# A two-layer trunk with expert lookups on one core: the latents' projection and layer 1's modulation change places, the prompt's ranking runs beside its queries, latents go in groups of 1, 1 and 2, and attention's copies move to ScalarE

## The chip, the cores and the metric

One NeuronCore of a Trainium2 chip runs the whole program. The metric is the device time of one execution in microseconds (us); the median of the runs counts. Engines: TensorE (PE, with its weight load PEld), VectorE (DVE), ScalarE (ACT), GpSimd (POOL) and SyncE (SP). SP and POOL issue transfers; 16 DMA engines carry them.

## The reference, cut to what matters

There are 5 tiles of 128 tokens: tile 0 is the prompt, tiles 1 to 4 are the latents. Both of the two layers run this sequence for every tile:

```python
m = silu(cond) @ w_mod + b_mod            # 6 rows of 1024: shift, scale, gate, shift, scale, gate
h = rms_norm(x) * (1 + scale) + shift
layer 0: p = h @ l0_w_in                  # 2080 columns: q, k, v, r, decay inputs, pool inputs
         y = concat(gla(p), pool(p)) @ l0_w_out
layer 1: q, k, v = h @ l1_w_in            # 1536 columns
         y = window_attention(q, k, v)    # 16 heads, +-128 tokens, cached context, a sink logit
x = x + gate * y                          # (layer 1: y is attention's output @ l1_w_out)
h = rms_norm(x) * (1 + scale2) + shift2   # PEER, the expert lookup:
s = (h @ w_q) . keys                      # 8 heads x 2 halves x 128 keys
top 16 of each half, top 16 of their sums # 128 experts a token, with softmax gates
act = gelu(u[expert] . h);  x = x + gate2 * sum(gates * act * v[expert])
```

GLA of a latent tile needs the states of all latent tiles, so the projection of all four comes before any of them is mixed.

## The kernel before, in words

**Experts in the background.** `Experts` keeps one sequence of 10 x 128 slots: layer, tile, and one of 128 experts per token. For each slot GpSimd issues an indirect DMA (L1928) that fetches 128 rows of 8 KB (`u` and `v` together) into a ring of 8 buffers (9 in layer 1). VectorE takes the dot product with `h` (L1945), ScalarE makes gelu, gate and, for slots that TensorE owns, a diagonal matrix (L1968, L1971, L1974); then either VectorE adds the weighted row (L1960) or TensorE does (L1985, `sum_rows`). A buffer is free again after that. GpSimd can't gather a tile before its selection is done: it waits on `selected`.

**Foreground and rates.** Everything else is a row of stages in program order. Each stage has units, and a rate tuple (rate, places on TensorE, lead). On entry the goal of processed slots rises by lead, and after unit u it stands at base + int(u x rate); every engine's program puts the slots' steps at those places. `bg.allow(n)` cuts the goal off at n x 128 slots. Before the first selection there are no slots, and the same mechanism (`core.fill = early`) fills the prolog with the steps of `Early`.

**The order before.** `modulation_stage` does the first 4 of 12 chunks of layer 0's modulation. Then come the prompt's norm, projection, decays, GLA, pool, output projection (`p0_out`), queries and selection. Beside them `Early` does 8 more chunks of layer 0's modulation (L358, L2135, L2149, L2156; weights by GpSimd, L2185) and then the norm (L2240, L2241, L2249) and the projection (L2262, L2226) of all four latent tiles. When both are done, the background starts. The latents' decays, GLA and pool of tile 1, its output projection, queries and selection (`s0a`) follow; then the same for tiles 2 to 4 together (`s0b`), with one pass over the weights `l0_w_out` and `peer_wq` and three selections. Then `mod1` does layer 1's modulation in 12 chunks. In layer 1 the prompt and tiles 1 and 2 are normed and projected together (`j1`), then come attention and the selections for the prompt and tile 1, and so on (`s1b`, `s1c`).

**Two details.** A selection (`select_stage`, 21 units) makes 16 score matmuls (L1748) and ranks all 16 rows in five passes (L1774 to L1782), then pairs and ranks the sums. In attention VectorE takes a head's maximum (L1638), negates it (L1645), ScalarE exponentiates (L1618), TensorE transposes (L1582), VectorE copies the transposed tile out of PSUM (L1652), and TensorE multiplies with the values (L1594). A pair of heads goes through at a time, with the background's slots between maxima and copies.

The main sequence of layer 0 before:

```python
early.finish()
core.fill = bg
bg.allow(1)
latent_decay_stage(core, "s0_decay", latents, pr, la, st, ahead, FIRST_RATES["decay"])
layer0_mix(core, "s0a", latents, [0], pr, la, st, constants, (BAND_FIRST, BAND_AFTER), FIRST_RATES)
first_experts(core, "s0a", first, 0, FIRST_RATES, None, 2, env["h"][:, others[0], :])
bg.allow(2)
layer0_mix(core, "s0b", latents, [1, 2, 3], pr, la, st, constants, (BAND_AFTER, BAND_BEFORE), REST_RATES)
other_experts(core, "s0b", latents[1:], 0, 1, REST_RATES)
```

## Time and profile before

| what | value |
|---|---|
| median of 3 runs | 4137.85 us (4133.88 to 4142.95) |
| profiled execution, its time | 4151.75 us |
| its span, first to last instruction | 4149.6 us |
| busy: PE, DVE, ACT, POOL | 2942.8, 3047.3, 1414.3, 1613.3 us |
| moved by DMA | 1521.91 MB, mean 367 GB/s |
| of it by the gathers' queue (q0) | 1366.06 MB |
| granted TensorE clock, mean | 0.848 |

A profile is one execution. The time minus the span (2 us) lies around the first and last instruction. Busy shares are means over stages with different limits, so they don't tell what a stage waits for. The granted clock is TensorE's share of 2.4 GHz.

### The profile page before, as it was taken

The numbers are of one execution on the slowest core, as the hardware profiler recorded it, in microseconds if no ns is written. First come the engines' busy times: TensorE is split into PE (matmuls) and PEld (weight loads), VectorE is DVE, ScalarE is ACT, GpSimd is POOL, SyncE is SP. The second block draws the span as 40 slices with busy tenths as digits, with TensorE's granted clock in tenths as the row PEclk, the third lists the DMA queues.
The fourth block names the chain that finished last, engine by engine and source line by source line (L and its number), as shares of the span: only waits on it lengthen the run. The fifth ranks groups of instructions, "written<-read, shape, count | busy, mean of one in ns | idle before, by whom it ended". The sixth has DMA issues, their size and how long they took to land.

```text
span 4149.6 us, 32638 instructions
## 1 busy us (share of the span) xinstructions
PE 2942.8 (71%) x9247; PEld 1520.7 (37%) x9247; DVE 3047.3 (73%) x6149; ACT 1414.3 (34%) x4109; POOL 1613.3 (39%) x1309
## 2 busy tenths in 40 slices
PE   6699756875877844757768877776787677755665
PEld 2365342444522311423446323344355533222222
DVE  1406779978897847697778886978797898666666
ACT  1213323522233312235522332542464233332222
POOL 0001332434544524344333553434544454444443
PEclk8798887987999966877879988888998899888888
DMA  9143897989998999899999999999999999999998
GB/s 363 57 169 144 330 397 271 344 338 357 416 393 368 396 404 382 329 396 404 366 381 403 406 382 390 385 386 419 411 408 410 419 407 381 422 422 414 418 422 365
DMA packets 222322, 1521.91 MB, mean 367 GB/s; under 512 B 29757, under 2 KB 33537, under 8 KB 48822
## 3 DMA queue, kind: packets, MB, share of 16 engines
q0 software_dynamic: 186912, 1366.06, 81.3%
q1 hardware_dynamic: 35230, 153.77, 9.4%
q8 instruction: 74, 1.21, 0.1%
q14 instruction: 106, 0.87, 0.1%
HBM read 1516.49 MB, written 3.24 MB: 366 GB/s over the span
## 4 chain that ended last, share of the span: by engine, by line
DMA 29%; PE 29%; DVE 24%; issue 8%; POOL 4%; ACT 4%; DVEq 1%; SPq 1%; PEldq 0%; PEld 0%; ACTq 0%
DMA core_ring<-in_l_uv,core_experts 24%; PE sum_rows L1985 7%; DVE core_ring L1945 7%; DVE core_yv L1960 5%; POOL core_ring L1928 4%; PE sum_rows L2262 2%; PE j_in_ps L490 2%; PE s1c_query_pq L1699 1%; PE s1b_in_ps L490 1%; DMA s0a_h_w<-in_l_peer_wq 1%; DMA layer_slot<-in_l_uv,core_experts 1%; PE j_query_pq L1699 1%; DMA mod_w<-in_l_w_mod 1%; PE s0b_out_po L629 1%; DVEq L159 1%
## 5 line engine op out<-in xcount | busy, mean ns | idle before, releaser
L1928 POOL DMA_INDIRECT core_ring<-in_l_uv,core_experts x1209 | 1515.2, 1253 | 2111.3 <-PE sum_rows L1985 974.9
L1985 PE MATMUL sum_rows<-core_ring,core_diag 128*128 128x512 f32 x2820 | 1533.8, 689 | 600.6 <-ACT core_diag L1974 477.1
L1945 DVE CUSTOM_DVE_ANT_0 core_ring<-core_ring,core_hc 128x1024 f32<-128x1024 f32 x1209 | 1465.0, 1223 | 583.0 <-DMA core_ring<-in_l_uv,core_experts 408.3
L1985 PEld LDWEIGHTS sum_rows<-core_ring,core_diag 128*128 128x128 f32 x2820 | 576.1, 217 | 1482.6 <-ACT core_diag L1974 792.2
L1968 ACT ACTIVATE core_wt<-core_wt 128x1 f32<-128x1 f32 x1280 | 256.3, 200 | 1660.0 <-DVE core_wt L1945 1566.8
L1960 DVE SCALAR_TENSOR_TENSOR core_yv<-core_ring,core_wt,core_yv 128x1024 f32<-128x1024 f32 x494 | 632.7, 1281 | 22.6 <-ACT core_wt L1971 22.1
L1971 ACT ACTIVATE core_wt<-core_wt,core_gates 128x1 f32<-128x1 f32 x1280 | 376.8, 294 | 41.6
L1974 ACT ACTIVATE core_diag<-core_ident,core_wt 128x128 f32<-128x128 f32 x705 | 283.1, 401 | 23.0
L1985 PE MATMUL sum_rows<-layer_slot,layer_diag 128*128 128x512 f32 x184 | 107.6, 715 | 44.8 <-ACT layer_diag L1974 34.0
L2262 PE MATMUL sum_rows<-core_ring 128*128 128x416 f32 x320 | 117.8, 528 | 5.2 <-DVEq L159 4.1
L1945 DVE CUSTOM_DVE_ANT_0 layer_slot<-layer_slot,core_hc 128x1024 f32<-128x1024 f32 x71 | 86.9, 1224 | 44.0 <-DMA layer_slot<-in_l_uv,core_experts 29.8
L1928 POOL DMA_INDIRECT layer_slot<-in_l_uv,core_experts x71 | 84.4, 1188 | 85.7 <-DVE core_yv L1960 40.6
L1968 ACT ACT_TABLE_LOAD x81 | 103.9, 1283 | 5.2 <-DVEq L159 3.8
L1945 DVE DVE_READ_ACCUMULATOR2_ANT core_wt<- 128x1 f32 x1280 | 104.4, 82 | 0.0
L1699 PE MATMUL s0b_query_pq<-s0b_h_hT,s0b_h_w 128*128 128x384 f32 x256 | 85.3, 497 | 5.4 <-DVEq L159 5.4
L2262 PEld LDWEIGHTS sum_rows<-core_ring 128*128 128x128 f32 x320 | 61.8, 196 | 57.3 <-issue 57.1
L2194 POOL DMA_DIRECT2D core_ring<-in_l_w_in x5 | 2.7, 536 | 206.1 <-PE sum_rows L2262 206.1
L1985 PEld LDWEIGHTS sum_rows<-layer_slot,layer_diag 128*128 128x128 f32 x184 | 38.5, 222 | 107.7 <-ACT layer_diag L1974 59.7
L358 PE MATMUL mod_pm<-mod_w,mod_c_silu 128*32 128x512 f32 x192 | 45.8, 972 | 38.0 <-DMA mod_w<-in_l_w_mod 38.0
L490 PE MATMUL j_in_ps<-j_in_w,j_atth_hT 128*128 128x384 f32 x192 | 65.1, 504 | 5.8 <-DMA j_in_w<-in_l_w_in 5.8
L1699 PE MATMUL j_query_pq<-s_att_pr,j_h_w 128*128 128x256 f32 x256 | 59.8, 393 | 8.1 <-DVEq L159 7.8
L1699 PEld LDWEIGHTS s0b_query_pq<-s0b_h_hT,s0b_h_w 128*128 128x128 f32 x256 | 49.8, 195 | 40.8 <-issue 8.2
(778 smaller groups left out, 3293.4 us busy)
## 6 DMA issues: line engine op xcount, KB each, us to landing
mod_w<-in_l_w_mod SPq DMA_DIRECT2D x16, 2048.0 KB, 12.5
core_ring<-in_l_uv,core_experts POOLq DMA_INDIRECT x1209, 11.9
core_ring<-in_l_w_mod POOLq DMA_DIRECT2D x6, 2048.0 KB, 11.0
s_mix_pr<-in_l_w_in SPq DMA_DIRECT2D x5, 1664.0 KB, 11.0
core_ring<-in_l_w_in POOLq DMA_DIRECT2D x5, 1664.0 KB, 10.5
p_h_w<-in_l_peer_wq SPq DMA_DIRECT2D x16, 512.0 KB, 4.5
s0a_h_w<-in_l_peer_wq SPq DMA_DIRECT2D x16, 512.0 KB, 12.9
s0b_h_w<-in_l_peer_wq SPq DMA_DIRECT2D x16, 512.0 KB, 8.0
```

Source lines behind the costliest of these rows:

```text
L159: dve.drain().then_inc(meeting, 1)
L358: mm = nc.tensor.matmul(out[lo:lo + 32, :], silu[:, k, :], w[:, k, :], start=(k < 4), stop=(k >= 4))
L490: mm = nc.tensor.matmul(ps[:, i % 4, 0:chunk], hT[:, k, t * P:(t + 1) * P], w[n % 2][:, k * chunk:(k + 1) * chunk], start=(k == 0), stop=( ...
L1699: mm = nc.tensor.matmul(pq[:, n % 2, 0:tok], queries.chunk(n)[:, k, :], hT[:, k, :], start=(k == 0), stop=(k == DK - 1))
L1928: nc.gpsimd.indirect_dma_start(self.slots[r], None, core.a[f"l{layer}_uv"], bass.IndirectOffsetOnAxis(ap=self.experts[:, t, n:n + 1], axis ...
L1945: nc.vector.tensor_tensor_reduce(self.slots[r][:, 0:D], self.slots[r][:, 0:D], self.hc[:], 1.0, 0.0, ALU.mult, ALU.add, self.wt[:, r:r + 1 ...
L1960: x = nc.vector.scalar_tensor_tensor(self.yv[:], self.slots[r][:, D:], self.wt[:, r:r + 1], self.yv[:], ALU.mult, ALU.add)
L1968: nc.scalar.activation(self.wt[:, r:r + 1], self.wt[:, r:r + 1], ACT.Gelu_apprx_tanh).then_inc(self.gelu_done, 1)
L1971: nc.scalar.activation(self.wt[:, r:r + 1], self.wt[:, r:r + 1], ACT.Copy, scale=gate).then_inc(self.wt_done, 1)
L1974: nc.scalar.activation(self.diags[r], self.core.env["ident"][:], ACT.Copy, scale=self.wt[:, r:r + 1]).then_inc(self.diag_done, 1)
L1985: mm = nc.tensor.matmul(self.py[:, c * 512:(c + 1) * 512], self.diags[r], self.slots[r][:, D + c * 512:D + (c + 1) * 512], start=(at == 0) ...
L2262: mm = nc.tensor.matmul(self.ps[:, i % 2 * 512:i % 2 * 512 + self.CH], self.hT[:, k, t * P:(t + 1) * P], w[:, k, :], start=(k == 0), stop= ...
```

## The change

- `Early` no longer norms and projects the latents. It does 20 chunks of modulation: layer 0's last 8 and all 12 of layer 1. `mod1` is gone. Readers of layer 1's rows wait for them (`wait_rows`).
- The latents' norm and projection are ordinary stages (`layer0_rows`, `s0`) after the background has started, in the slots of tile 0, with rates of their own.
- The prompt's selection: `query_stage` makes the scores of a half head right behind its queries and ranks four rows at a time; the selection has 16 units left.
- Latents in layer 0 go as tile 1, tile 2 (`s0b`, by `first_experts`), tiles 3 and 4 (`s0c`), so `l0_w_out`, `peer_wq` and the keys are loaded three times for the latents and not twice.
- In attention the copy of the transposed tile is ScalarE's, behind its background slots of the pair; it was VectorE's.
- Rates of the prolog and of layer 0 are set anew.

```diff
@@ attention_stage, scalar
+            def take_turned(n):
+                keys, _ = keys_of(which[n // QH])
+                act.wait_ge(tr_done, n + 1)
+                if n >= 2:
+                    act.wait_ge(o_mm, n - 1)
+                nc.scalar.activation(pT[:, n % 2, 0:len(keys), :], ptr[:, n % 2, 0:len(keys), :], ACT.Copy).then_inc(pT_done, 1)
...
                 if n % 2:
                     s.tick("scalar", act, n + 1)
+                    take_turned(n - 1)
+                    take_turned(n)
@@ attention_stage, vector
-            def take_turned(n):
...
-                take_turned(n)
-                take_turned(n + 1)
@@ query_stage, tensor
+            def score(n):
+                if n == 0:
+                    pe.wait_ge(keys_in, 32)
+                pe.wait_ge(qT_done, n + 1)
+                nc.tensor.matmul(ranking.scores[:, n, :], qT[:, n, 0:P], keys[:, n * NKEYS:(n + 1) * NKEYS], start=True, stop=True
+                                 ).then_inc(ranking.scored, 1)
...
+                if n and ranking:
+                    score(n - 1)
@@ query_stage, vector
+            def rank(first):
+                rows = range(first, first + ROWS_AT_ONCE)
+                dve.wait_ge(ranking.scored, first + ROWS_AT_ONCE)
...
+                if ranking and n >= ROWS_AT_ONCE + 1 and (n - 1) % ROWS_AT_ONCE == 0:
+                    rank(n - 1 - ROWS_AT_ONCE)
+            if ranking:
+                rank(HC - ROWS_AT_ONCE)
@@ Early
-    MOD_STEPS, MOD_FIRST, MOD_CH, MOD_CHUNKS = 11, 4, 512, 12
-    STEPS = MOD_STEPS + 29
+    MOD_FIRST, MOD_CH, MOD_CHUNKS = 4, 512, 12
...
+        self.chunks = [(0, n) for n in range(self.MOD_FIRST, self.MOD_CHUNKS)] + [(1, n) for n in range(self.MOD_CHUNKS)]
+        self.rows = [(layer, n // 2) for layer, n in self.chunks[::2]]
+        self.STEPS = len(self.chunks) + 3
@@ Early.load, gpsimd
+            for n in range(2, chunks):
+                pool.wait_ge(self.mod_mm, n - 1)
+                pool.dma_start(self.mod_w[n % 2], self.weights(n)).then_inc(self.mod_w_in[n % 2], 16)
+                if n >= 5 and n % 2:
+                    store((n - 5) // 2)
+            for i in range(len(self.rows) - 2, len(self.rows)):
+                store(i)
+            for i in range(len(self.rows)):
+                pool.wait_ge(self.stored[i], 16)
@@ rates
-EARLY_RATES = {"norm": (0.0, None, 0), "in": (1.6, None, 2), "decay": (1.0, None, 1), "gla": (1.0, None, 1), "pool": (1.0, None, 1),
-               "out": (0.5, None, 2), "query": (0.0, None, 0), "select": (0.6, None, 1)}
+EARLY_RATES = {"norm": (0.0, None, 0), "in": (1.6, None, 2), "decay": (1.0, None, 1), "gla": (0.65, None, 0), "pool": (1.0, None, 0),
+               "out": (0.34, None, 1), "query": (0.0, None, 0), "select": (0.15, None, 0)}
-FIRST_RATES = {"norm": (2.0, PE_4, 5), "decay": (2.0, PE_8, 0), "gla": (1.6, PE_6, 4), "pool": (2.0, PE_2, 4),
-               "out": (1.7, PE_0, 3), "query": (1.0, PE_0, 2), "select": (0.8, PE_8, 3)}
-REST_RATES = {"norm": (3.0, PE_4, 5), "gla": (2.0, PE_6, 4), "pool": (2.0, PE_2, 4), "out": (1.75, PE_0, 3), "query": (2.0, PE_0, 2),
-              "first select": (1.5, PE_8, 3), "select": (2.1, PE_8, 3)}
+FIRST_RATES = {"norm": (2.0, PE_4, 5), "in": (1.9, PE_0, 4), "decay": (2.0, PE_8, 0), "gla": (1.6, PE_6, 4), "pool": (2.0, PE_2, 4),
+               "out": (1.7, PE_0, 3), "query": (1.0, PE_0, 2), "select": (1.1, PE_8, 3)}
+SECOND_RATES = {"gla": (2.0, PE_6, 4), "pool": (2.0, PE_2, 4), "out": (1.9, PE_0, 3), "query": (1.15, PE_0, 2), "select": (1.8, PE_8, 3)}
+REST_RATES = {"gla": (2.0, PE_6, 4), "pool": (2.0, PE_2, 4), "out": (1.9, PE_0, 3), "query": (1.25, PE_0, 2),
+              "first select": (2.0, PE_8, 3), "select": (2.1, PE_8, 3)}
@@ program
-            ahead = Ahead(core, latents)
-            first_experts(core, "p0", 0, 0, EARLY_RATES, ahead)
+            first_experts(core, "p0", 0, 0, EARLY_RATES, ranked=True)
             early.finish()
             core.fill = bg
             bg.allow(1)
+            ahead = Ahead(core, latents)
...
+            layer0_rows(core, "s0", latents, pr, None, (), FIRST_RATES, ahead.load)
...
-            layer0_mix(core, "s0b", latents, [1, 2, 3], pr, la, st, constants, (BAND_AFTER, BAND_BEFORE), REST_RATES)
-        other_experts(core, "s0b", latents[1:], 0, 1, REST_RATES)
-        with Stage(core, "mod1_c") as m:
-            modulation_stage(core, 1, "mod1", m.sb("silu", [P, DK, 32])[:], early.MOD_CHUNKS, [1, 4], 2, (2.5, PE_0, 3))
+            layer0_mix(core, "s0b", latents, [1], pr, la, st, constants, (BAND_AFTER, BAND_BEFORE), SECOND_RATES)
+            first_experts(core, "s0b", latents[1], 0, SECOND_RATES, 2, env["h"][:, latents[2], :])
+            bg.allow(3)
+            layer0_mix(core, "s0c", latents, [2, 3], pr, la, st, constants, (BAND_AFTER, BAND_BEFORE), REST_RATES)
+        other_experts(core, "s0c", latents[2:], 0, 2, REST_RATES)
```

## Rows read from the trace of the kernel before

**Rows 1.** The page: GB/s moved in 40 equal slices of the span.

```profile
GB/s 363 57 169 144 330 397 271 344 338 357 416 393 368 396 404 382 329 396 404 366 381 403 406 382 390 385 386 419 411 408 410 419 407 381 422 422 414 418 422 365
```

**Rows 2.** Busy time by stretch: length, each engine, clock, DMA share, GB/s.

```profile
0.00:373.00 373.00, 292.61 (x1257) 165.43 (x1258) 107.74 (x322) 64.75 (x109) 11.97 (x26) 0.87 0.44 169
276.00:306.00 30.00, 29.19 (x257) 28.66 (x256) 0.00 (x0) 4.43 (x16) 0.00 (x0) 1.00 0.65 215
373.00:423.00 50.00, 41.38 (x164) 24.11 (x163) 30.35 (x54) 33.05 (x61) 19.02 (x18) 0.76 0.83 317
423.00:500.00 77.00, 54.49 (x257) 28.39 (x255) 61.81 (x102) 31.67 (x73) 22.86 (x21) 0.86 0.80 303
500.00:615.00 115.00, 68.86 (x352) 54.48 (x352) 78.82 (x102) 26.77 (x88) 39.58 (x32) 0.81 0.98 400
615.00:692.00 77.00, 49.27 (x105) 19.20 (x106) 74.95 (x267) 23.46 (x71) 24.49 (x20) 0.80 0.82 311
692.00:872.00 180.00, 140.40 (x691) 70.68 (x690) 160.83 (x276) 87.74 (x194) 59.99 (x52) 0.91 0.81 307
1450.00:1655.00 205.00, 87.51 (x268) 22.82 (x267) 118.20 (x161) 38.77 (x128) 69.83 (x49) 0.67 0.97 395
1655.00:1705.00 50.00, 34.42 (x67) 15.25 (x66) 30.21 (x42) 21.26 (x48) 14.07 (x12) 0.65 0.58 219
1705.00:1780.00 75.00, 66.05 (x195) 37.90 (x193) 51.80 (x66) 15.48 (x56) 32.67 (x24) 0.95 1.01 423
1780.00:2095.00 315.00, 216.48 (x592) 108.14 (x593) 259.88 (x465) 160.62 (x447) 138.13 (x116) 0.77 0.96 388
2095.00:2250.00 155.00, 114.34 (x446) 87.00 (x444) 113.46 (x142) 38.76 (x118) 54.16 (x45) 0.84 0.98 391
2250.00:2370.00 120.00, 94.00 (x215) 40.21 (x216) 103.92 (x317) 45.65 (x147) 60.49 (x47) 0.93 0.99 399
2370.00:2500.00 130.00, 100.55 (x220) 41.36 (x219) 107.54 (x320) 45.76 (x148) 65.38 (x49) 0.89 0.97 390
3600.00:4050.00 450.00, 276.31 (x445) 95.84 (x446) 304.07 (x430) 133.93 (x470) 212.05 (x179) 0.83 1.01 419
```

**Rows 3.** The chain that ended last, 300 to 373.5 us: start, length.

```profile
315.59 55.88 PE sum_rows L2262 x160
```

**Rows 4.** Groups of instructions, 0 to 373 us: busy us, mean ns | idle before.

```profile
L2262 PE MATMUL sum_rows<-core_ring 128*128 128x416 f32 x320 | 117.8, 528 | 5.2 <-DVEq L159 4.1 <-ACTq L154 0.6 <-PEq L164 0.5
...
L358 PE MATMUL sum_rows<-core_ring 128*32 128x512 f32 x128 | 18.2, 641 | 5.0 <-DMA core_ring<-in_l_w_mod 2.6 <-ACTq L154 1.4 <-ACT core_ring L2149 1.0
...
L2240 DVE SCALAR_TENSOR_TENSOR core_h<-core_x,core_wt,core_ring 128x1024 f32<-128x1024 f32 x4 | 5.1, 1284 | 0.1
```

**Rows 5.** Instructions in order of time, end of the prolog: start, length.

```profile
315.63 3.26 DVE L1774 MAX8 p_select_vals<-p_select_pscore 128x8 f32<-128x128 f32 x16 [8.06 <-PE p_select_pscore L1748]
...
335.22 0.29 DVE L1790 CAST p_select_idxf<-p_select_i 128x256 f32<-128x256 uint32 x1
...
361.03 0.29 DVE L1836 TENSOR_TENSOR core_gates<-p_select_ts,p_select_gs 128x128 f32<-128x128 f32 x1
...
373.15 1.00 POOL L1928 DMA_INDIRECT core_ring<-in_l_uv,core_experts  x1 [45.36 <-issue]
```

**Rows 6.** The page: DMA issues, KB each, median us from issue to landing.

```profile
core_ring<-in_l_uv,core_experts POOLq DMA_INDIRECT x1209, 11.9
...
s0a_h_w<-in_l_peer_wq SPq DMA_DIRECT2D x16, 512.0 KB, 12.9
```

**Rows 7.** Waits, 3000 to 3190 us: us in total, times, longest.

```profile
ACT s1c_attend_sc L1618 <- DVE s1c_attend_mx L1645: 40.8, 16, 6.8
```

**Rows 8.** Groups of instructions, 3000 to 3190 us: busy us, mean ns.

```profile
L1652 DVE COPY s1c_attend_pT<-s1c_attend_ptr 128x512 f32<-128x512 f32 (+1 forms) x32 | 18.3, 613 | 0.0
...
L1618 ACT ACTIVATE s1c_attend_sc<-s1c_attend_sc,s1c_attend_mx 128x512 f32<-128x512 f32 (+1 forms) x32 | 21.4, 669 | 40.8 <-DVE s1c_attend_mx L1645 40.8
...
L1618 ACT ACT_TABLE_LOAD x16 | 20.5, 1283 | 5.0 <-DVE s1c_attend_mx L1645 4.7
```

281 lines of the change are left out of this document (124 added, 157 removed).

## The prediction

> **What bounds the kernel now.** I read the page's row of bytes moved first: after the first tenth of the span the DMA engines move 330 to 420 GB/s nearly everywhere, and only the start has holes [rows 1]. Then busy time by stretch, in stretches cut at the stages: in the free-running end 179 gathers take 450 us at 419 GB/s and a DMA share of 1.01, so one slot (128 expert rows, 1.05 MB) costs 2.51 us and DMA sets the pace there; VectorE is busy 304 of the 450 us [rows 2]. At that rate the whole 1,522 MB would take about 3,620 us of the 4,149.6; the rest is time in which DMA moves less. The largest hole is the prolog: 169 GB/s over 373 us is 63 MB, 150 us of work, so some 222 us are lost before the first gather [rows 2]. The chain shows why: its last piece there is 55.88 us of the latents' projection (L2262), which follows the prompt's selection [rows 3]; the order in time shows gates ready at 361.3 us and the first gather at 373.15 [rows 5].
>
> **The prolog.** The latents' projection is 320 matmuls and 117.8 us of TensorE [rows 4]. Half lies in the last piece [rows 3]; the other 61.9 us stands between the prompt's own steps. Of it I take 58 us off the way to the prompt's gates (an estimate: some 4 us lay under w_out's flight). The latents' norm leaves too: four times two VectorE passes of 1.28 us, 10 us, in the middle of the prompt's GLA [rows 4]. The ranking: the first top-16 over 16 rows runs from 315.63 to 335.22, 19.6 us after the queries [rows 5]. Now three quarters of it lie beside the queries, where VectorE is busy 0.00 us [rows 2] (7 us of queries per 4.9 us of ranking), and one quarter stays: -15 us. The scores' matmuls move, they don't go: 0.
>
> Added: 12 more chunks of modulation. Eight cost 18.2 us of TensorE, 2.3 us each [rows 4], and each has a fold of two more matmuls, at their mean of 641 ns 1.3 us: 43 us in all. Below nothing is excluded; all of it on the path is the upper bound. Much of it falls where TensorE waits for the prompt's exponentials and norms, so I take 25. Their 25.2 MB (60 us) fit into a prolog that has 222 us free; each chunk needs 5 us of DMA and is due every 8 or 10 us. TensorE now has holes where the projection kept it busy: the granted clock was 1.00 (2.4 GHz) during the prompt's queries and 0.87 over the whole prolog, so part of it ran at 1.2 GHz [rows 2]; for the prompt's output and query stages I add 6 us (bounds 0 and 20). The queue of GpSimd gets 8 more small loads ahead of its first chunk, hidden behind the norm's start, and the last store before the first gather: 2 us. Sum: 361.3 - 58 - 10 - 15 + 25 + 6 + 2 = 311; the gather at 312 instead of 373: -61 us.
>
> **From there to layer 1, by slot goals.** A stage moves the goal of gathered slots by its lead plus int(units x rate), cut off at the limit. By the old rates layer 0's last selection ends at 342, and the old kernel reaches the joined norm (1655 us) at 387 slots. The new ones: norm 5 + 4 x 2.0 = 13, projection 13 + 4 + 20 x 1.9 = 55, decay 67, GLA 83, pool 89, output 102, queries 120, selection cut off at 128; then second latent tile GLA 148, pool 154, output 168, queries 188, selection 228; then the last two 264, 272, 297, 319, 364, 411.
>
> Times by the nearest stretch. Norm of four tiles: like the joined one, 50 us for 12 gathers [rows 2], plus 12 for the first rows' flight (11.9 us median [rows 6]), less 6, an estimate, because two rows of the modulation are spread over the partitions and not four: 56. Projection: 42 slots and 8.7 MB, 52.8 MB at the 423 GB/s of the joined projection [rows 2] = 125, with one weight load ahead 128; TensorE's 117.8 us lie under it. Decay 48, GLA and pool 77, output and queries 115, as before [rows 2]. Selection of the first latent tile: 77 us with 20 gathers before; now only 8 slots are left, VectorE needs 45 us of its own (315.6 to 361.3 [rows 5]), 8 dots and TensorE's scores: 62. DMA has nothing to fetch for some 50 of these, since the next tile's indices are what is being computed; VectorE then waits about 10 us for the first row. Second tile: GLA and pool 82 + 12, output and queries 127 (34 slots against 32 gathers in 115), selection 108 (47 gathers took 120, less ten slots of 1.2 us on VectorE). Last two: GLA 120 (two thirds of the 180 us for three tiles) and pool 22, output and queries 163 (45 gathers took 155), selections 117 and 117 (47 gathers took 120) [rows 2]. From 312 this gives 1666 us with 411 slots, where the old kernel has 1655 with 387: 11 us late, 24 slots ahead. In it is a third pass over layer 0's output and query weights: 4 x 1 MB by the code and 16 x 0.5 MB [rows 6], with keys and band 15 MB, 36 us at full rate. It also holds what goes: layer 1's modulation was part of the 205 us from 1450 with only 49 gathers [rows 2].
>
> The joined stages up to the queries keep their durations (315 + 155 us and the norm's 50 and projection's 75 [rows 2]). They now start at 411, so the next selection enters at 609 and hits the limit of 640 two thirds through. It takes 88 us for 31 slots instead of 120 for 47 gathers; about 20 us of DMA idleness lie in its tail. The second one then starts with empty slots: 138 instead of 130. That sums to 2487 us at 687 slots; before, 2500 at 678. 13 us and 9 slots x 2.5 us: 35 us ahead. From here both have the same stages and the same slots to go.
>
> **Attention's copies.** VectorE loses 32 copies of 613 ns in the last attention stage [rows 8] and 80 over the 40 pairs of heads; at the same cost that is 49 us, the bound of a gain, since most of these stretches run near DMA's rate [rows 2]. ScalarE takes them up between the experts' weights and the next exponentials. There it waited 40.8 us for VectorE's maxima in 16 pairs, 2.5 us each [rows 7]. Two copies take about 1.3 us on either engine (no ScalarE copy of this form is in the trace; its exponentials of the same tile are the nearest, 669 ns [rows 8]), and the maxima come 1.3 us sooner: cover and need are even, the exponentials start when they did, and VectorE is freer. I take -4 us; bounds -49 and +51 (the fourth rival).
>
> **Sum.** Against its own time of 4,151.75 us the profile gives -35 - 4 = -39, so 4,113. Profiled executions stand 14 us above the median of the three runs (4,137.85), and I carry that over: 4,099. With 3 us for the joins between stages, which the stretches cut coarsely: 4,102.
>
> **Rivals.** *The selection starves less, or the added weights fall into idle DMA.* For it: stretches with GLA run at 303 to 307 GB/s [rows 2], so any load there is free. Against: the output and query stretches run at 400. If half of the 36 us and 10 of the 50 idle us are free, and the chunks cost 15 instead of 25: 4,102 - 38 = 4,064. *The prolog shrinks by less.* If 35 of the chunks' 43 us are on the path and the clock costs 15: 19 us less, 4,121. For it: the L358 matmuls waited for their loads in the old prolog too [rows 4]. Against: the new chunks are due further apart. *Moved, not removed.* Weights (36 us), the starved selections (50 + 20 against some 25 lost before) and a slower norm eat the prolog's 61: 4,138; it needs about 35 us beyond my stage times. *Slower: ScalarE's order in attention.* The copies stand before a table load that so far ran during the wait (1,283 ns [rows 8]). If it is not covered any more, copies 1.3 + load 1.28 - maxima 1.3 = 1.28 us later per pair; TensorE releases ring rows only behind the exponentials' transposes, so gathers stop meanwhile: 51 us over 40 pairs in place of my -4, 4,157. It decides from 1.2 us per pair on. Against it: the 2.5 us of cover was measured behind the load [rows 7]. The Trainium skill (ScalarE: Activation LUTs, Table sets: the hidden batching unit) says that every set holds the plain copy, and that each change of set is budgeted at about 2.7 us. The row's 1.28 us does not bear the 2.7 out, and the measurement decides; by the page's figure this rival would cost some 57 us more, 4,214, an estimate from that page.
>
> **How the numbers follow.** Forecast 0.44 (its own range 4,085 to 4,120); larger gain 0.20; smaller prolog gain 0.14; moved, not removed 0.10; slower by attention 0.12. Its chance is held down by the cover. 0.2% (8 us) is what a measurement of this kernel can tell from no change. Faster: 0.44 + 0.20 + 0.14 and little of the fourth, 0.79; same 0.08; slower 0.13. The range goes from beyond the larger gain, 4,056, to short of the slower rival, 4,150, which leaves out some 0.1 on each side.
>
> **What would show it.** The first gather near 312 us and no pause of L358 matmuls for DMA in the prompt's GLA; the latents' projection at over 400 GB/s; a hole of some 50 us in the DMA row during the first latent tile's selection and one of 20 in the joined stage's; no modulation stretch before layer 1; attention stretches within 3 us of before with ScalarE's wait near zero. I am wrong if the gather comes after 330, if the hole is longer than the selection, or if attention's stretches grow.

## The result, and the profile after

| | before | after |
|---|---|---|
| median of 13 runs each, on shared chips | 4139.48 us (4129.38 to 4149.95) | 4157.02 us (4144.29 to 4168.05) |
| profiled execution: time, span | 4151.75, 4149.6 us | 4160.44, 4158.7 us |
| first gather | 373.15 us | 351.39 us |
| moved by DMA | 1521.91 MB | 1536.14 MB |

The ratio after to before is 1.0038, 95% interval 1.0025 to 1.0051: the change makes the kernel 16 us slower by the ratio and 18 by the medians. The forecast was 4102, faster. 4157 lies outside its range (4056 to 4150).

The page of the changed kernel, GB/s in 40 slices [rows 1]:

```profile
GB/s 357 202 193 201 375 297 333 320 268 384 415 343 332 399 412 398 317 405 395 392 408 381 393 348 405 385 405 393 421 411 402 419 411 386 422 421 419 413 422 373
```

Where before had 57 in its second slice, and 271 only in its seventh, there are now 193 to 202 in the prolog, 268 in the ninth slice (832 to 936 us), and 343 and 332 in the twelfth and thirteenth. Busy time by stretch, columns as in [rows 2]; from 351 us on the last number in brackets, GpSimd's, is the count of gathers. The stretches are: the prolog, the prompt's queries, latents' norm, projection, decay, GLA and pool, output and queries, first latent selection, second tile, last two tiles, joined norm, joined selections, free-running end:

```profile
0.00:351.00 351.00, 223.50 (x1119) 113.93 (x1119) 108.48 (x326) 50.78 (x87) 21.92 (x45) 0.78 0.58 223
281.00:311.00 30.00, 30.00 (x258) 30.00 (x258) 11.54 (x72) 3.88 (x14) 0.00 (x0) 0.95 0.55 176
351.00:427.00 76.00, 27.05 (x64) 12.89 (x64) 42.03 (x57) 23.70 (x56) 25.06 (x23) 0.63 0.85 337
427.00:546.00 119.00, 113.53 (x320) 61.46 (x320) 90.77 (x114) 26.99 (x96) 43.72 (x37) 0.97 0.93 379
546.00:608.00 62.00, 48.29 (x175) 26.96 (x176) 34.02 (x58) 36.12 (x68) 17.16 (x15) 0.72 0.58 218
608.00:684.00 76.00, 57.42 (x266) 29.60 (x264) 63.80 (x107) 32.73 (x77) 25.00 (x22) 0.87 0.85 330
684.00:793.00 109.00, 62.55 (x343) 51.85 (x341) 73.66 (x94) 25.29 (x83) 36.39 (x30) 0.83 0.98 398
793.00:876.00 83.00, 25.55 (x68) 13.16 (x69) 68.34 (x251) 14.71 (x39) 13.06 (x11) 0.64 0.47 189
876.00:1178.00 302.00, 205.77 (x812) 118.54 (x812) 243.32 (x517) 100.89 (x300) 124.21 (x100) 0.88 0.95 383
1178.00:1735.00 557.00, 416.73 (x1394) 228.00 (x1392) 460.34 (x1000) 198.15 (x573) 230.99 (x185) 0.87 0.95 376
1735.00:1796.00 61.00, 32.76 (x65) 14.34 (x64) 30.32 (x39) 17.97 (x43) 15.98 (x16) 0.66 0.64 251
2326.00:2548.00 222.00, 163.60 (x376) 69.50 (x376) 192.84 (x608) 78.24 (x249) 105.98 (x82) 0.89 0.92 374
3600.00:4050.00 450.00, 274.52 (x457) 96.37 (x456) 298.03 (x424) 134.21 (x470) 213.61 (x177) 0.85 1.01 419
```

The prolog now moves 223 GB/s instead of 169, but its TensorE is busy 223.5 us instead of 292.6 and it is only 22 us shorter. The forecast had it 61 us shorter. Behind it, the stretch of the first latent selection (793 to 876) moves 189 GB/s where before it moved 311. Its gates are ready at 850.3, after 57 us; the rest of the stretch is the ring's refilling and the next stage's start:

```profile
850.03 0.29 DVE L1895 TENSOR_TENSOR core_gates<-s0a_select_ts,s0a_select_gs 128x128 f32<-128x128 f32 x1
```

The joined norm starts at 1735, where the forecast said 1666 and before was at 1655. The free-running end is as before.

The chain that ended last, 281 to 365 us (start, length), answers to [rows 3]. No projection stands in it any more. For 71 us the view names no releaser ("issue"); behind them stands the store of the last modulation row, and then the gather:

```profile
277.09 71.36 issue
...
348.47 1.79 DMA mods<-core_ring
```

Groups of instructions, 0 to 351 us: busy us, mean ns of one | idle before [rows 4]:

```profile
L358 PE MATMUL sum_rows<-core_ring 128*32 128x512 f32 x320 | 64.6, 790 | 10.3 <-DMA core_ring<-in_l_w_mod 8.1 <-ACTq L154 1.4 <-ACT core_ring L2246 0.8
L2232 PE MATMUL sum_rows<-core_ring,core_fold 128*2 128x512 f32 x40 | 27.6, 780 | 43.2 <-DVE core_ring L2255 19.2 <-DVE core_h L2255 11.0 <-DVE core_h L2259 6.0
```

Twenty chunks take 64.6 us of TensorE, 3.2 each, where eight took 2.3 each [rows 4]: one product has a mean of 790 ns instead of 641. With the fold (L2232, 27.6 us, 1.4 each) a chunk takes 4.6 us and the twelve new ones take 55; the prediction had 3.6 and 43.

In order of time, the prompt's gates and the first gather, answering to [rows 5]. The gates end at 347.4; the gather comes 4.0 us later, behind the last store:

```profile
347.12 0.29 DVE L1895 TENSOR_TENSOR core_gates<-p_select_ts,p_select_gs 128x128 f32<-128x128 f32 x1
...
351.39 1.01 POOL L1987 DMA_INDIRECT core_ring<-in_l_uv,core_experts  x1 [2.41 <-issue]
```

The first weights of the latents' projection, from the view of one tile (first and last issue), and what TensorE waited for:

```profile
L481 SPq DMA_DIRECT2D s_in_w<-in_l_w_in x5: 327/328/908, 409.6 to 496.4; - x5
...
  DMA s_in_w<-in_l_w_in: 40.6, 2
```

The 40.6 us are one wait counted twice, 20.7 for the weight load and 19.9 for the product. The first weights are issued at 409.6, behind the norm, and the projection starts at 427.6 us.

### The profile page after: what moved, and what is told of

Same layout as the page of the kernel before. It is cut to its first block, busy times and chain, and to the rows that moved or that the text cites. A ratio compares the mean times of both kernels' runs of the same rounds, so it can differ in the third digit from the quotient of the medians.

```text
span 4158.7 us, 33203 instructions
## 1 busy us (share of the span) xinstructions
PE 2902.4 (70%) x9427; PEld 1546.6 (37%) x9427; DVE 3041.8 (73%) x6091; ACT 1441.8 (35%) x4187; POOL 1603.4 (39%) x1328
## 2 busy tenths in 40 slices
DMA packets 224384, 1536.14 MB, mean 369 GB/s; under 512 B 28590, under 2 KB 32882, under 8 KB 50116
## 4 chain that ended last, share of the span: by engine, by line
DMA 29%; PE 29%; DVE 24%; issue 9%; ACT 4%; POOL 4%; DVEq 1%; PEldq 0%; SPq 0%; PEld 0%; ACTq 0%; POOLq 0%
DMA core_ring<-in_l_uv,core_experts 21%; PE sum_rows L2044 8%; DVE core_ring L2004 6%; DVE core_yv L2019 4%; POOL core_ring L1987 3%; PE s_in_ps L492 3%; PE j_in_ps L492 2%; PE s0c_query_pq L1726 1%; DMA layer_slot<-in_l_uv,core_experts 1%; PE s1c_query_pq L1726 1%; DVEq L159 1%; DMA s0a_h_w<-in_l_peer_wq 1%; PE sum_rows L358 1%; PE s1b_in_ps L492 1%; DMA j_h_w<-in_l_peer_wq 1%
## 5 line engine op out<-in xcount | busy, mean ns | idle before, releaser
L1987 POOL DMA_INDIRECT core_ring<-in_l_uv,core_experts x1209 | 1492.4, 1234 | 2113.8 <-DVE core_yv L2019 988.5
L2044 PE MATMUL sum_rows<-core_ring,core_diag 128*128 128x512 f32 x2720 | 1470.9, 687 | 617.0 <-ACT core_diag L2033 422.2
L2044 PEld LDWEIGHTS sum_rows<-core_ring,core_diag 128*128 128x128 f32 x2720 | 554.9, 217 | 1450.8 <-ACT core_diag L2033 715.5
L2019 DVE SCALAR_TENSOR_TENSOR core_yv<-core_ring,core_wt,core_yv 128x1024 f32<-128x1024 f32 x519 | 664.9, 1281 | 25.2 <-ACT core_wt L2030 24.8
L2033 ACT ACTIVATE core_diag<-core_ident,core_wt 128x128 f32<-128x128 f32 x680 | 273.0, 402 | 22.2
L492 PE MATMUL s_in_ps<-s_in_w,s_mixh_hT 128*128 128x416 f32 x320 | 113.5, 518 | 19.9 <-DMA s_in_w<-in_l_w_in 19.9
L2027 ACT ACT_TABLE_LOAD x83 | 106.5, 1283 | 52.1 <-DVEq L159 30.8
L492 PEld LDWEIGHTS s_in_ps<-s_in_w,s_mixh_hT 128*128 128x128 f32 x320 | 61.5, 192 | 72.1 <-issue 51.4
L358 PE MATMUL sum_rows<-core_ring 128*32 128x512 f32 x320 | 64.6, 790 | 10.3 <-DMA core_ring<-in_l_w_mod 8.1
L1726 PE MATMUL s1c_query_pq<-s1c_h_hT,s1c_h_w 128*128 128x256 f32 x256 | 57.3, 388 | 5.6 <-DVEq L159 5.6
L1726 PE MATMUL s0c_query_pq<-s0c_h_hT,s0c_h_w 128*128 128x256 f32 x256 | 57.3, 388 | 5.4 <-DVEq L159 5.4
## 6 DMA issues: line engine op xcount, KB each, us to landing
s_in_w<-in_l_w_in SPq DMA_DIRECT2D x5, 1664.0 KB, 11.3
```

Of the source, the lines that this page charges most:

```text
L358: mm = nc.tensor.matmul(out[lo:lo + 32, :], silu[:, k, :], w[:, k, :], start=(k < 4), stop=(k >= 4))
L492: mm = nc.tensor.matmul(ps[:, i % 4, 0:chunk], hT[:, k, t * P:(t + 1) * P], w[n % 2][:, k * chunk:(k + 1) * chunk], start=(k == 0), stop=( ...
L1726: mm = nc.tensor.matmul(pq[:, n % 2, 0:tok], queries.chunk(n)[:, k, :], hT[:, k, :], start=(k == 0), stop=(k == DK - 1))
L1987: nc.gpsimd.indirect_dma_start(self.slots[r], None, core.a[f"l{layer}_uv"], bass.IndirectOffsetOnAxis(ap=self.experts[:, t, n:n + 1], axis ...
L2019: x = nc.vector.scalar_tensor_tensor(self.yv[:], self.slots[r][:, D:], self.wt[:, r:r + 1], self.yv[:], ALU.mult, ALU.add)
L2027: nc.scalar.activation(self.wt[:, r:r + 1], self.wt[:, r:r + 1], ACT.Gelu_apprx_tanh).then_inc(self.gelu_done, 1)
```

## The experiments

Differences are taken from ratios to before, each measured in 5 rounds on shared chips; 0.1% is 4.1 us. The diffs show the main lines only. The same prolog has its first gather at 341.8 to 351.4 us in five profiles (the changed kernel and experiments 2, 6, 7 and 12; mean 347.7), so a single profile places it within some 5 us. In these five the prompt's gates end at 343.7 in the mean, and the last store takes the 4.0 us behind them.

**1 and 2. Attention's copies alone.** Into the kernel before, and out of the changed one:

```diff
-                nc.vector.tensor_copy(pT[...], ptr[...]).then_inc(pT_done, 1)
+                nc.scalar.activation(pT[...], ptr[...], ACT.Copy).then_inc(pT_done, 1)
```

> The kernel before with one part of the change alone: the turned probabilities of each pair of heads are copied out of PSUM by ScalarE instead of VectorE. Theory (what the trace of the changed kernel shows of its attention stages, 21 us shorter together, is this part's own): the first gather stays at 373 us, the joined prompt's attention about as before, s1a_attend and s1c_attend some 8 to 12 us shorter each, the whole 12 to 20 us shorter than before (ratio 0.995 to 0.997). Rival (the stages are shorter in the changed kernel only because its gathers stand elsewhere): within 5 us of before. Rival of the prediction (the copies in ScalarE's order cost more than they free): 10 us or more above before.

> The changed kernel with the attention's copies back on VectorE. Theory: 12 to 20 us above the changed kernel, that is 4169 to 4177 against 4157 (ratio to before 1.007 to 1.009), all of it in the four attention stages; nothing ahead of 2000 us moves. Rival (the copies are worth nothing): 4157 again.

Measured: 4126.88 us, ratio 0.9961 (0.9945 to 0.9978), 16 us faster than before; and 4170.16, ratio 1.0064 (1.0045 to 1.0083), 11 us slower than the changed kernel. The first is as the theory has it, the second just short of it (1.007 to 1.009). Busy time in the attention of the first latent tile and of the last two, first in the kernel before, then in experiment 1:

```profile
1984.00:2098.00 114.00, 87.30 (x308) 51.22 (x307) 89.03 (x165) 61.08 (x165) 42.71 (x39) 0.82 0.92 368
...
2997.00:3193.00 196.00, 163.42 (x653) 101.79 (x653) 172.51 (x317) 121.78 (x323) 87.02 (x75) 0.87 0.99 403
```

```profile
1970.00:2072.00 102.00, 81.26 (x305) 47.04 (x305) 82.84 (x149) 66.98 (x181) 43.28 (x39) 0.90 0.99 405
...
2965.00:3158.00 193.00, 165.63 (x653) 100.91 (x653) 156.45 (x285) 135.69 (x355) 84.59 (x75) 0.87 1.00 409
```

VectorE is busy 16 us less in the longer stretch, ScalarE 14 us more, and 39 slots go through the first in 102 us instead of 114. The waits and groups of the changed kernel's last attention stage, 3044 to 3232 us, answer to [rows 7, 8]:

```profile
ACT s1c_attend_sc L1627 <- DVE s1c_attend_mx L1656: 10.4, 11, 3.2
```

```profile
L1627 ACT ACTIVATE s1c_attend_sc<-s1c_attend_sc,s1c_attend_mx 128x512 f32<-128x512 f32 (+1 forms) x32 | 21.4, 668 | 10.7 <-DVE s1c_attend_mx L1656 10.4
L1627 ACT ACT_TABLE_LOAD x16 | 20.5, 1283 | 5.6 <-DVE s1c_attend_mx L1656 5.4
```

The copies by form, VectorE's before (3000 to 3190 us) and ScalarE's in the changed kernel:

```profile
L1652 DVE COPY s1c_attend_pT<-s1c_attend_ptr 128x512 f32<-128x512 f32 x16 | 10.2, 679 | 0.0
L1652 DVE COPY s1c_attend_pT<-s1c_attend_ptr 128x384 f32<-128x384 f32 x16 | 8.1, 547 | 0.0
```

```profile
L1619 ACT ACTIVATE s1c_attend_pT<-s1c_attend_ptr 128x512 f32<-128x512 f32 x16 | 8.5, 582 | 0.0
L1619 ACT ACTIVATE s1c_attend_pT<-s1c_attend_ptr 128x384 f32<-128x384 f32 x16 | 6.8, 475 | 0.0
```

ScalarE's wait for the maxima fell from 40.8 to 10.4 us and did not turn into a delay.

**3 and 4. The chunks, and the ranking.**

```diff
-        self.chunks = [(0, n) ...] + [(1, n) for n in range(self.MOD_CHUNKS)]
+        self.chunks = [(0, n) ...]
...
-            first_experts(core, "p0", 0, 0, EARLY_RATES, ranked=True)
+            first_experts(core, "p0", 0, 0, EARLY_RATES)
```

The first two lines are experiment 3, which leaves layer 1's modulation out altogether; the last two are experiment 4.

> The changed kernel with the twelve chunks of layer 1's modulation left out (its rows hold the bias alone, so layer 1 is computed with wrong rows; 25 MB of weights are not read either). Theory (each of the twelve chunks costs the prompt's path some 5 us, because its fold, its copy and its sums stand in series with the prompt's own work): the first gather comes at 290 to 298 us instead of 351.4 and the whole is 50 to 60 us under the changed kernel, near 4100. Rival (my prediction's 25 us for the twelve, and the missing rest of the gain is elsewhere in the prolog): first gather at 323 to 330, the whole near 4130.

> The changed kernel with the prompt's ranking back behind its queries, in its selection. Theory (the ranking beside the queries does what it says and its 21 us of VectorE ran in the shadow of TensorE's query products but for 6.7 us): first gather 14 to 18 us later, at 366 to 369, the whole 10 to 18 us above the changed kernel. Rival (the chunks that ride in the same stretch set its end anyway): first gather within 4 us of 351.4, the whole as the changed kernel.

Measured: 4113.84, ratio 0.9927 (0.9906 to 0.9948), 46 us under the changed kernel, first gather at 301.19; and 4168.77, ratio 1.0053 (1.0034 to 1.0072), about 6 us above it with the intervals overlapping, first gather at 354.02.

```profile
301.19 1.01 POOL L1987 DMA_INDIRECT core_ring<-in_l_uv,core_experts  x1 [176.91 <-DVE core_gates L1895]
```

Twelve chunks cost 347.7 - 301.2 = 46 us, 3.9 each, between the theory's 5 and the forecast's 2.1. Four of the 46 are the last store behind the gates: in experiment 3 the gather follows its gates (300.9) at once. The ranking is worth 6 us at the first gather, not 15, and 354.02 lies within the rival's 4 us of 351.4. At the gates it is worth more: they end at 353.8 in experiment 4, 10 us after the mean of 343.7, but there the last store is through before them.

**5 and 6. The other moves taken back.** Layer 1's modulation as a stage again; the latents as 1 and 3.

```diff
-        self.chunks = [(0, n) ...] + [(1, n) for n in range(self.MOD_CHUNKS)]
+        self.chunks = [(0, n) ...]
+        with Stage(core, "mod1_c") as m:
+            modulation_stage(core, 1, "mod1", ..., (1.0, PE_0, 3))
...
-            layer0_mix(..., [1], ...); first_experts(core, "s0b", ...); layer0_mix(..., [2, 3], ...)
+            layer0_mix(core, "s0b", latents, [1, 2, 3], ...)
```

> The changed kernel with layer 1's modulation back as a stage of its own between layer 0 and layer 1 (its fill rate 1.0 slot a chunk), the rest as changed. From the run without the twelve chunks: first gather at 298 to 304 us (47 us sooner). Theory (the 25 MB then pass in a stretch where the DMA engines are the bound, so the stage costs 60 us of them, and the prolog's 47 us are paid back): the whole within 15 us of the changed kernel's 4157, more likely above. Rival (the stage fills holes in the DMA that the main part has anyway, as in the joined norm with its 25 us lost): 4120 to 4140, near the run without the chunks.

> The changed kernel with the latents' last three tiles in one group again (as before; fill rates of that part lowered by 15% so that the 128 slots that the selections have freed last). 14 MB less are read. Theory (the extra pass of output and query weights is 34 us of a DMA-bound stretch and buys nothing): 4120 to 4135, 22 to 37 us under the changed kernel. Rival (an earlier selection of tile 1 keeps the gathers fed, and one group runs out of slots at its first selection): within 8 us of 4157 or above it.

Measured: 5 gives 4211.51, ratio 1.0154 (1.0134 to 1.0174), 48 us slower than the changed kernel, beyond both expectations. Its first gather is at 302.41, as expected. What costs is the stage, and behind it the slot limit; stretches of the stage and of the joined selections:

```profile
1690.00:1806.00 116.00, 53.28 (x220) 10.29 (x220) 47.31 (x65) 15.80 (x47) 14.29 (x15) 0.69 0.91 368
2390.00:2595.00 205.00, 133.38 (x316) 56.54 (x316) 175.70 (x578) 65.03 (x206) 83.71 (x67) 0.88 0.81 331
```

The stage takes 116 us for 15 gathers, and 15 slots at 2.51 us [rows 2] would need 38. The joined selections then hit the limit of 640 slots sooner and move 331 GB/s instead of 374; that part, 24 us (205 x 331 / 374 is 181), belongs to my fill rate and not to the move. So layer 1's modulation in the prolog is a gain here, not the loss that I had made of it: 46 us paid, and 94 saved behind the prolog, or 70 without my fill rate's part.

6 gives 4152.68, ratio 1.0027 (1.0016 to 1.0039), 5 us under the changed kernel, inside the rival's 8. The 14 MB saved come back as a starved stretch, the three tiles' GLA, at a DMA share of 0.74 (0.81 before [rows 2]). The edit also lowered that part's fill rates by some 15%, so the 5 us are the grouping and the rates together:

```profile
867.00:1028.00 161.00, 133.92 (x671) 69.44 (x670) 147.01 (x258) 81.11 (x174) 50.02 (x43) 0.90 0.74 272
```

**7. The projection's weights ahead.** Two buffers of their own, loaded behind the modulation rows while the norm runs.

```diff
+        if first is None:
+            first = HeldWeights(core, t)
+            behind = (first.load,)
         norm_stage(core, f"{tag}_norm", tiles, 0, hT, rates["norm"], behind)
```

> The changed kernel with the first two weight chunks of the latents' projection loaded into buffers of their own while the latents' norm runs. Theory (the 18 us that the projection waits at its start for a chunk queued behind gathers are on the path of the first window, which is short of slots and not of DMA): projection starts at 408 to 415 us instead of 427.6, the selection of the first latent tile ends 10 to 17 us sooner, the whole 8 to 17 us under the changed kernel. Rival (the norm stretches by what its DMA now shares, or the gain is lost in the hole of the selection): within 5 us of 4157.

Measured: 4138.42, ratio 0.9990 (0.9979 to 1.0001), 20 us under the changed kernel, slightly more than the theory. In the profile the projection's start is 18.6 us earlier and the first selection ends 15 us earlier. Norm and projection:

```profile
365.00:409.00 44.00, 27.09 (x60) 12.92 (x60) 30.34 (x40) 19.71 (x44) 11.02 (x11) 0.64 0.80 312
409.00:526.00 117.00, 111.90 (x321) 60.62 (x319) 98.53 (x125) 28.58 (x102) 52.27 (x42) 0.99 1.01 417
```

**8. Copies and ranking in the kernel before**, projection still in the prolog.

> The kernel before with two parts of the change: the attention's copies on ScalarE and the prompt's ranking beside its queries; the projection stays in the prolog, layer 1's modulation a stage, the latents as 1 and 3. Theory (parts add up: 16.5 us for the copies, 9 to 12 us for the ranking): first gather at 361 to 365 us instead of 373, the whole 4112 to 4120, 24 to 30 us under before (ratio 0.993). Rival (before, the prolog's fill sets the end of the selection and the ranking is hidden already): first gather at 370 to 375, the whole as the first experiment, 4127.

Measured: 4138.18, ratio 0.9987 (0.9978 to 0.9996): 11 us slower than experiment 1 without the ranking. The theory of parts that add up fell, and the rival too, which had the whole as in experiment 1. The chain and the first gather:

```profile
344.73 37.38 PE sum_rows L2320 x107
```

```profile
383.78 1.01 POOL L1986 DMA_INDIRECT core_ring<-in_l_uv,core_experts  x1 [45.36 <-issue]
```

L2320 is the latents' projection there. Gates were ready at 362.9 us, but the gather waited for the projection, which is the prolog's end whatever the ranking does. That the ranking pushed the projection's steps back is the likely reason for the 8 us by which the gather is later than in experiment 1 (375.50); it isn't shown.

**9. The projection moved, alone.** The changed kernel with ranking and copies off, the modulation stage back at 2.5 slots a chunk, and the latents as 1 and 3. It is not quite alone: the prolog and the first window keep the changed kernel's rates, and the last three tiles have experiment 6's lowered ones.

> The kernel before with one part of the change alone, the latents' norm and projection out of the prolog: no ranking, no copies on ScalarE, layer 1's modulation a stage again (2.5 slots a chunk), the latents as 1 and 3. Theory (this part is the one that loses: it takes some 63 us out of the prolog and puts 190 us of norm and projection into a first window that has only 128 slots to gather): first gather at 308 to 318 us, the first latent selection's end at 830 to 850 us (before 694) with all 128 slots long gone, the whole 4190 to 4240, so 50 to 95 us above before (ratio 1.011 to 1.023). Rival (additive in the other direction: the part is neutral by itself and the loss is the chunks' and the grouping's): 4130 to 4160.

Measured: 4212.95, ratio 1.0158 (1.0138 to 1.0178), 65 us slower than before, as the theory has it. First gather at 313.35. The prolog, and the first latent selection:

```profile
0.00:313.00 313.00, 179.41 (x903) 105.84 (x903) 96.80 (x309) 43.96 (x74) 8.27 (x19) 0.75 0.44 169
...
761.00:846.00 85.00, 29.23 (x69) 15.09 (x70) 69.32 (x252) 15.80 (x41) 13.07 (x11) 0.60 0.47 189
```

The prolog is 60 us shorter, and the first window, from the first gather to the first latent selection's end, is 533 us instead of 320 (373 to 693 [rows 2]). Both have the prompt's 128 slots to gather, 321 us at 2.51 each. Before, 91 were gathered by then (18 + 21 + 32 + 20 [rows 2]) and 37 were left for what follows; now the selection gets 11 gathers and the DMA engines stand half idle. But part of the 65 us lies behind the window. The next stages of the same kind, experiment 9 first and before second:

```profile
1005.00:1560.00 555.00, 402.63 (x1138) 212.38 (x1136) 442.69 (x1099) 163.78 (x512) 226.11 (x181) 0.87 0.91 362
```

```profile
872.00:1450.00 578.00, 426.46 (x1194) 223.37 (x1193) 481.31 (x1154) 179.18 (x570) 266.91 (x203) 0.89 0.95 384
```

At before's 384 GB/s the 555 us would be 523. So some 32 of the 65 us, an estimate from these two rows, were lost where the edit had lowered the rates too, and projection and rates are not separated there.

**10. Layer 1's chunks in the prolog of the kernel before**, between layer 0's and the projection, with the copies on ScalarE and no stage between the layers.

> The kernel before with the attention's copies on ScalarE and with layer 1's twelve modulation chunks in the prolog behind layer 0's eight, the latents' norm and projection still in the prolog after them, no modulation stage between the layers, latents as 1 and 3. Theory (the chunks cost the prolog 4 us each and take 25 MB, 60 us of the DMA's bound, out of the main part): first gather at 418 to 435 us instead of 375, the whole 4095 to 4125, 2 to 30 us under the first experiment's 4127. Rival (with both fills the prolog's TensorE is full and each chunk costs 5 us or more, the stage between the layers filled holes): 4127 to 4150.

Measured: 4127.48, ratio 0.9965 (0.9951 to 0.9978), the same as experiment 1. The first gather comes at 444.57, 69 us after experiment 1's 375.50: 5.8 us a chunk, beyond the theory's 4 and as the rival has it (5 or more, and a whole from 4127 on). What the prolog pays, the main part gives back: some 67 us, near experiment 5's 70.

**11. The chunks' products taken out.** Layer 1's twelve chunks make one small product each instead of their sums, so its rows hold wrong numbers.

```diff
+                if self.chunks[n][0]:
+                    nc.tensor.matmul(self.ps[:, 0:64], ident, self.mod_w[n % 2][:, 0:64], ...)
+                else:
                     quarter_sums(...)
```

> The changed kernel with each of layer 1's twelve chunks cut to one small product of 64 columns in place of its eight quarter sums (wrong rows for layer 1; weights, fold, ScalarE's copy, VectorE's sum, semaphores and stores all stay). The trace has 3.2 us of TensorE for the eight quarter sums of a chunk. Theory (the twelve cost the prompt's path their TensorE time, as it stands in the order between the prompt's own products): first gather 30 to 38 us sooner, at 313 to 321, the whole 4120 to 4130. Rival (they cost it their waits: weights not yet there, fold, copy and sum in series): first gather within 12 us of 351, the whole 4148 to 4157.

Measured: 4138.65, ratio 0.9998 (0.9989 to 1.0007), 17 us under the changed kernel. Groups 0 to 340 us, and the gather:

```profile
L2239 PE MATMUL sum_rows<-core_ring,core_ident 128*128 128x64 f32 x24 | 7.3, 399 | 4.1 <-DMA core_ring<-in_l_w_mod 4.1
```

```profile
334.25 1.01 POOL L1987 DMA_INDIRECT core_ring<-in_l_uv,core_experts  x1 [2.55 <-issue]
```

L358 has 20.4 us left. By groups 37 us of products went (64.6 - 20.4 - 7.3). TensorE as a whole was busy 21 us less, 202.75 instead of 223.50, since groups overlap and some of the prompt's own products took longer (mean clock 0.76 against 0.78):

```profile
0.00:334.00 334.00, 202.75 (x951) 110.79 (x951) 108.57 (x326) 50.96 (x87) 21.93 (x45) 0.76 0.61 234
```

The first gather gains 13 us (347.7 to 334.3), give or take the 5 of a profile. That is between the theory's 30 to 38 and the rival's 12 at the most. So 33 of the 46 us stay when the sums are gone, while the fold, the copy, the addition and the handoffs between them are left.

**12. Fewer slots early**, on top of 7: 1.0 instead of 2.0 a unit in the decay stage, 1.2 instead of 1.6 in GLA.

> The changed kernel with the projection's first weights loaded ahead (as in the seventh experiment, 4138) and fewer fill slots before the first latent selection: 1.0 instead of 2.0 a unit in the decay stage, 1.2 instead of 1.6 in the gated linear attention, so that some 10 slots more are left for the selection, where the DMA engines stood idle for 47 of 84 us. Theory (the first window is bound by the foreground's own steps, so slots moved from a stage with DMA idle to another change nothing by themselves, but the decay and attention stages lose a few us with fewer copies on VectorE): selection's DMA loss down by 20 us, its end 0 to 8 us sooner, the whole within 8 us of 4138. Rival (the hole in the selection is what the change loses): 4110 to 4125.

Measured: 4130.44, ratio 0.9973 (0.9961 to 0.9985), 7 us under experiment 7 with the intervals overlapping, within the theory's 8. Decay, GLA to queries, selection, of 7 and of 12:

```profile
526.00:588.00 62.00, 48.17 (x175) 26.82 (x176) 33.65 (x57) 36.12 (x68) 17.40 (x15) 0.72 0.60 223
588.00:776.00 188.00, 122.00 (x606) 82.77 (x604) 137.85 (x200) 57.73 (x159) 60.59 (x51) 0.84 0.92 365
776.00:861.00 85.00, 27.73 (x70) 14.76 (x70) 69.45 (x252) 14.77 (x39) 13.06 (x11) 0.64 0.47 188
```

```profile
529.00:581.00 52.00, 40.36 (x154) 24.75 (x154) 28.57 (x50) 34.16 (x56) 9.38 (x9) 0.67 0.51 183
581.00:759.00 178.00, 114.36 (x598) 79.40 (x597) 131.51 (x189) 53.08 (x147) 57.16 (x48) 0.86 0.90 358
759.00:853.00 94.00, 48.17 (x106) 19.39 (x105) 79.58 (x269) 22.54 (x65) 23.49 (x20) 0.73 0.67 268
```

Nine slots moved into the selection fill its hole (268 GB/s instead of 188), and yet the three stretches together are only 11 us shorter: the hole was a symptom of a foreground too long for its slots, as the theory says. Experiment 12's gates of the first latent tile are ready 8 us sooner.

**13 and 14. The fold one step later**, alone, and with 12's edits.

```diff
-            if 2 <= n < chunks + 2:
-                i = n - 2
+            if 3 <= n < chunks + 3:
+                i = n - 3
```

> The changed kernel with each chunk's fold one step later in the prolog's fill, and VectorE's sum one step after it, so that TensorE's fold waits for a sum that VectorE passed a unit earlier (the trace of the changed kernel has TensorE idle for 21 us before folds in the stretch 125 to 351, waiting for VectorE's sums, without one 19 us wait at the end of it that has nothing behind it). Theory (half of what the chunks cost beyond TensorE's own time is this wait): first gather 8 to 20 us sooner than 346 to 351, the whole 4137 to 4149. Rival (the rest of the cost lies in the stages' ends, where every fill step up to there has to be through before the prompt goes on, and a longer chain makes that no shorter): first gather at 344 to 356, the whole 4150 to 4162.

> The changed kernel with three edits together: the projection's first weights ahead, fewer fill slots early (both as in the twelfth experiment, 4130), and the fold one step later. Theory: 4130 less what the later fold gives by itself, 4110 to 4122. Rival (the later fold gives nothing): 4130.

Measured: 4177.48, ratio 1.0088 (1.0069 to 1.0107), and 4151.28, ratio 1.0010 (0.9997 to 1.0024): each 15 to 21 us slower than its base, with first gathers at 361.53 (347.7 without) and 373.44 (350.95 in 12). Both expectations were wrong on the same side: the fold's wait for VectorE is no cost that this takes away, and with the fold and the addition a step later the first gather comes 14 to 22 us later. At the prompt's gates it is 11 and 15 us (354.3 and 362.4 against 343.7 and 346.9); the rest is the last rows' end behind the gates, 7.2 and 11.1 us where it was 4.0.

**15 and 16. The chunks beside the selection**, on the changed kernel and on 12's.

```diff
-  "gla": (0.65, None, 0), "pool": (1.0, None, 0), "out": (0.34, None, 1), ..., "select": (0.15, None, 0)
+  "gla": (0.45, None, 0), "pool": (0.5, None, 0), "out": (0.17, None, 0), ..., "select": (0.5, None, 0)
```

> The changed kernel with the prolog's fill shifted: 0.45 instead of 0.65 steps a unit in the prompt's linear attention, none in its pooling, 0.17 instead of 0.34 in its output projection, and 0.5 instead of 0.15 in its selection, so that some five of the twelve chunks stand beside the selection's VectorE work, where TensorE has nothing of the prompt's to do. Theory (what a chunk costs is the handoffs of one step, sums, copy, fold, addition, at a place where the prompt's own steps are as short as it; beside a selection it is hidden): queries start 18 to 25 us sooner, at 252 to 260, the selection gets 5 to 15 us longer, first gather at 332 to 342, the whole 4140 to 4150. Rival (VectorE waits in its order for each fold, so the selection grows by the same 4 to 5 us a chunk or more): first gather 345 to 365, the whole 4155 to 4175.

> The twelfth experiment's kernel (4130: projection's weights ahead, fewer fill slots early) with the same shift of the prolog's fill. Theory: 4113 to 4123. Rival: 4128 to 4148.

Measured: 4149.29, ratio 1.0025 (1.0015 to 1.0036), 5 us under the changed kernel, first gather at 339.32; and 4122.38, ratio 0.9956 (0.9941 to 0.9970), 7 us under experiment 12 and 18 us faster than before. Of 16 only the time is known, not the first gather. In both pairs the intervals overlap. In 15 the queries start at 264.0 instead of 279.3, less soon than the theory's 252 to 260, and the selection takes 7 of these 15 us back. Gather and whole are as the theory has them (332 to 342, 4140 to 4150), and so is 16 (4113 to 4123).

## Why the prediction was wrong

**The step that failed** is the term of the twelve chunks, +25 us on the way to the first gather, at most 43: they cost 46. With it went the claim that the prolog's gain would reach the end; what had been moved behind the prolog took longer than its terms. In the profile the forecast (4,113) is 47 us short of 4,160: 39 in the prolog and 30 from the first gather to the joined norm (1,384 us against 1,354), less 22 that the rest won. The remaining 8 us of the 55 between 4102 and 4157 lie in two small terms. I carried over that a profiled execution stands 14 us above the median; the changed kernel's stands 3.4 above it. And I had added 3 us for joins. One small sum was off too, with nothing hanging on it: at 419 GB/s the 1,522 MB take 3,632 us, not 3,620.

**The first gather: 312 forecast, 347.7 the mean of five profiles (351.4 the one shown).** Three terms of the sum, by experiments 9, 3, 5 and 4:
- *Projection and norm out, with the clock and the store: -60 from the gates at 361.3.* Experiment 9 has the gather at 313.35: -48. Two reasons are likely, and their shares aren't shown: of the 61.9 us of projection that stood between the prompt's steps not all was on the way, and the granted clock fell, 0.75 over experiment 9's prolog against 0.87 [rows 2].
- *Ranking: -15.* From experiment 9 (313.35) to experiments 3 and 5 (301.19, 302.41) it is -11.5, and with the chunks in (experiment 4) -6, because the last store then comes behind the gates. It does run beside the queries.
- *Twelve chunks: +25.* Measured: 46. I took the chunk's cost to be its TensorE time, bounded it by that time from above, and let it hide in part. Both halves were off. The bound of 43 stood on before's means (641 ns a product, 3.6 us a chunk); in the changed kernel the chunks take 4.6 us each, 55 in all, so 46 is above my bound but not above their TensorE time. And little of it hid: I had taken 25 of 43. Nor does the cost follow that time alone: with the sums gone in experiment 11, 13 of the 46 us go and 33 stay, while TensorE is busy 21 us less. Experiment 13 puts the fold a step later and the prolog grows; experiment 15 puts chunks beside VectorE's selection and gets 8 us. Together they say that steps and place count beside TensorE's time. Which handoff carries how much isn't settled.

313.35 - 11.5 + 46 gives 347.8, the measured 347.7 by construction: the terms are differences between neighbouring runs. Against the forecast they are 12, 3.5 and 21 us.

**Norm and projection, 56 and 128 forecast, 76 and 119** (at 379 GB/s, where my sign was over 400). For the first weight load I had 3 us (125 to 128). But the code issues it behind the norm, at 409.6, and the projection waits until 427.6; the tile's five loads have a median of 11.3 us. That this one stood behind gathers is likely, not shown. Experiment 7 takes this out: start at 409 instead of 427.6, and 20 us of the total.

**The first selection, 62 forecast.** This held: its gates are ready after 57 us, with the 8 slots and nothing left to fetch, and GpSimd waited 51.0 us for them. The stretch of 83 us reaches into what the forecast counted with the second tile; together they take 385 us (793 to 1178) against 62 + 94 + 127 + 108 = 391. What I did not see is where such a hole comes from: experiment 9 puts 190 us of foreground into a window that has 321 us of gathers. The losses of this part are decay, 62 instead of 48, of which experiment 12 gets 10 back by taking slots out, and the last two tiles, 557 instead of 539, which no run explains.

**The third pass over weights, 36 us at full rate.** Experiment 6 puts 1, 1, 2 against 1, 3 at 5 us, lowered rates included: its 14 MB cost little in a part that is short of slots. Here I was probably too high.

**Layer 1's modulation.** The forecast named it only as a part of the 205 us from 1450, with no term of its own. Behind the prolog its going is worth some 70 us in experiment 5 (94 with the fill rate's part) and 67 in experiment 10. In the prolog it costs 46 without the projection and 69 beside it, so it is a gain of 24 to 48 us in the first case and none in the second.

**Attention, -4 forecast; -16 and -11 measured.** Right mechanism, size off: VectorE's freedom was worth more. ScalarE's 128x512 copy takes 582 ns where VectorE's took 679, and ScalarE's wait fell to 10.4 us, not to the near zero of my sign. The rival with the table load did not come: the loads are still 16 of 1,283 ns, and ScalarE still waited for maxima behind them. The Trainium skill's 2.7 us for each change of set (ScalarE: Activation LUTs, Table sets: the hidden batching unit) does not show on the path here.

**The account in parts,** from ratios: the projection moved +65; the copies -11 to -16; the ranking about -6; grouping +5; layer 1's modulation would have to make up the rest of the measured +16, which needs -32 to -37 and lies within its 24 to 48. This is a fit and no proof: experiment 8 showed that parts don't simply add, the +65 and the +5 hold lowered rates, and the change's new rates were never tried alone. Two of my rivals came true together. "The prolog shrinks by less" (0.14) had 35 us for the chunks and 15 for the clock. "Moved, not removed" (0.10, 4138) was right in kind, but I had it fed by 36 us of weights, the cheapest part, and left out the 20 of the late load. That it could end slower than before I had given only to attention, which was the part that gained.

**What the runs found:** experiment 16, the change with its projection's weights loaded ahead, fewer slots early and chunks beside the selection, has ratio 0.9956. Experiment 1, the old order with the copies alone, has 0.9961. The intervals all but coincide, so the reordering, as far as it was tried, is worth nothing measurable over a move of one copy.

## What to carry to other kernels

When work leaves a starved prolog for a stretch with a background of gathers, count the slots that the stretch has against its foreground: before moving 190 us in, it had 320 us of foreground for 321 us of gathers, weights not counted, and 37 of the 128 slots were left at its end. Price filler work by its chain of handoffs and by what stands beside it, and take its engine time from rows at the clock that it will find: 3.6 us a chunk before, 4.6 after. Look up where the first load of a moved stage is issued, and behind what it queues.
